# Batching the modulation rows of a two-layer diffusion block, four weight tiles to one accumulator copy

## The reference, cut to what matters

```python
def adaln(cond, w_mod, b_mod):
    return jnp.split(jax.nn.silu(cond) @ w_mod + b_mod, 6, axis=-1)

for l in range(DEPTH):
    sh1, sc1, g1, sh2, sc2, g2 = [m[:, None, :] for m in adaln(c, w_mod[l], b_mod[l])]
    csh1, csc1, cg1, csh2, csc2, cg2 = adaln(c_ctx, w_mod[l], b_mod[l])
    a_lat = rmsnorm(h, norm1_g[l]) * (1.0 + sc1) + sh1
    ...                     # token mixer: Fourier branch and state-space branch, gates, w_out
    h = h + g1 * o_lat
    f_lat = rmsnorm(h, norm2_g[l]) * (1.0 + sc2) + sh2
    h = h + g2 * channel_mixer(l, f_lat, ...)   # layer 0: dense SwiGLU; layer 1: top 2 of 8 experts
    ...                     # layer 0: the same for the context z, with csh1 to cg2
return rmsnorm(h, final_g)
```

## Time and profile before

| what | value |
|---|---|
| median of 3 runs | 2270.03 us (2267.54 to 2272.53) |
| the profiled execution's own time | 2270.69 us |
| its span in the profile | 2268.9 us |
| TensorE busy (products) | 2145.1 us, 95% of the span |
| DVE busy | 1400.2 us, 62% |
| ACT busy | 932.0 us, 41% |

### The profile page before, as it was taken

The page is one execution under the profiler, slowest core; times in us unless marked ns, Lnnn a source line. Parts: engine busy times, 40 slices in busy tenths (PEclk is TensorE's granted clock), DMA queues, the critical chain, the costliest instruction groups (busy, mean ns, idle before and its releaser), DMA issues.

```text
span 2268.9 us, 26156 instructions
## 1 busy us (share of the span) xinstructions
PE 2145.1 (95%) x10092; PEld 1618.4 (71%) x10092; DVE 1400.2 (62%) x1857; ACT 932.0 (41%) x839; POOL 0.2 (0%) x4
## 2 busy tenths in 40 slices
PE   4999989898999999899997999999999999999995
PEld 1455475345777777668986888888888888888884
DVE  5566516744222323418036889888888888888885
ACT  1212102111221222111004776767676766767673
POOL 0000000000000000000000000000000000000000
PEclk9999968998999999999697999999999999999997
DMA  8413574521435441357325999999898999999893
GB/s 355 112 75 149 172 171 179 183 74 37 182 143 194 164 194 48 133 159 176 97 108 215 359 348 355 353 335 377 330 374 325 369 341 360 350 338 378 325 374 150
DMA packets 84588, 536.49 MB, mean 236 GB/s; under 512 B 23040, under 2 KB 50304, under 8 KB 52992
## 3 DMA queue, kind: packets, MB, share of 16 engines
q1 hardware_dynamic: 62688, 513.89, 61.9%
q10 hardware_dynamic: 21792, 21.01, 2.8%
HBM read 516.59 MB, written 18.28 MB: 236 GB/s over the span
## 4 chain that ended last, share of the span: by engine, by line
PE 91%; DMA 4%; DVE 3%; issue 1%; ACT 1%; SPq 0%; DVEq 0%; ACTq 0%
PE ps L1486 20%; PE ps L1799 14%; PE ps L1800 14%; PE ps L1809 13%; PE ps L1495 6%; PE ps L1499 6%; PE ps L1502 5%; PE ps L1633 2%; PE ps L1422 2%; DMA bps<-BWs 2%; PE ps L1731 2%; PE ps L1753 1%; PE ps L1618 1%; DMA brt<-in_brt 1%; PE ps L1745 1%
## 5 line engine op out<-in xcount | busy, mean ns | idle before, releaser
L1326 DVE TENSOR_TENSOR WL<-mring,WH 128x2048 fp32r<-128x2048 f32 x340 | 763.6, 2288 | 111.9 <-ACT WH L826 111.4
L826 ACT ACTIVATE WH<-mring 128x2048 fp32r<-128x2048 f32 x340 | 632.6, 1913 | 142.2 <-PE ps L1809 130.2
L1799 PE MATMUL ps<-WH,XGh 128*128 128x512 f32 x896 | 358.2, 400 | 6.4 <-issue 3.9
L1800 PE MATMUL ps<-WH,XGl 128*128 128x512 f32 x896 | 349.9, 391 | 0.0
L1486 PE MATMUL ps<-aT,ring 128*128 128x512 f32 (+1 forms) x768 | 274.5, 518 | 12.4 <-ACT aT L707 12.4
L1486 PEld LDWEIGHTS ps<-aT,ring 128*128 128x128 f32 x768 | 147.8, 194 | 133.4 <-issue 122.0
L1809 PE MATMUL ps<-WL,XGh 128*128 128x512 f32 x896 | 221.5, 389 | 0.0
L1799 PEld LDWEIGHTS ps<-WH,XGh 128*128 128x128 f32 x896 | 168.9, 188 | 42.0 <-issue 5.1
L1809 PEld LDWEIGHTS ps<-WL,XGh 128*128 128x128 f32 x896 | 168.2, 188 | 34.9
L1800 PEld LDWEIGHTS ps<-WH,XGl 128*128 128x128 f32 x896 | 169.0, 189 | 33.6
L1151 DVE TENSOR_TENSOR ringl<-ring,FWH 128x4096 fp32r<-128x4096 f32 (+2 forms) x19 | 73.4, 3863 | 185.4 <-ACT FWH L693 185.4
(11 more groups left out here) (241 smaller groups left out, 2252.3 us busy)
## 6 DMA issues: line engine op xcount, KB each, us to landing
mring<-in_moe_gate SPq DMA_DIRECT2D x58, 2048.0 KB, 9.5
mring<-in_moe_up SPq DMA_DIRECT2D x57, 2048.0 KB, 9.7
mring<-in_moe_down SPq DMA_DIRECT2D x56, 2048.0 KB, 9.5
ring<-in_w_mod SPq DMA_DIRECT2D x24, 2048.0 KB, 8.3
ring<-in_w_in SPq DMA_DIRECT2D x12, 2048.0 KB, 11.8
ring<-in_ffn_gu SPq DMA_DIRECT2D x11, 2048.0 KB, 10.2
cks<-CW ACTq DMA_DIRECT2D x16, 512.0 KB, 3.3
ring<-cks SPq DMA_DIRECT2D x4, 2048.0 KB, 14.6
```

The lines of the kernel that those rows point to most:

```text
L826: nc.scalar.activation(WH[buf][:, o], mring[t % MRING][:, o], ACT.Copy).then_inc(high_done, 1)
L1326: V.tensor_tensor(WL[buf][:, o], mring[t % MRING][:, o], WH[buf][:, o].bitcast(F32), ALU.subtract).then_inc(low_done, 1)
L1799: mm(out_, ah, WH[buf][:, o:o + 512], start=(first and q == 0), stop=False)
L1800: mm(out_, al, WH[buf][:, o:o + 512], start=False, stop=False)
```

## The change

The selector and the sums are widened from two rows to eight. `silu4` holds four copies of the two condition columns, the i-th at columns 2i and 2i + 1 of an otherwise zero block of eight. Tile t uses block t mod 4 as stationary operand (128 x 8), so its two result rows land in rows 2(t mod 4) and 2(t mod 4) + 1 of each column group, and it adds zero to the others. The first tile of four starts the accumulation and the fourth ends it. ACT copies bank 2 once for four tiles, and one set of four turn products with a 128 x 8 selector makes the 32 columns. `mrow` has one buffer where it had two. DVE clears `silu4` at the start, and ACT applies `silu` four times, once into each block. The waits are counted in fours.

```diff
@@ constants @@
-        c[:, C_SEL + j] = p % 32 == j
+    c[:, C_SEL:C_SEL + 8] = (p[:, None] % 32) == np.arange(8)[None, :]
@@ tiles @@
-        mrow = sb(top, "mrow", [P, 2, 512])
+        mrow = sb(top, "mrow", [P, 512])
+        silu4 = sb(early, "silu4", [P, KD, 4, 8])
@@ ACT @@
-            nc.scalar.activation(silu_c[:], silu_c[:], ACT.Silu).then_inc(silu_c_ready, 1)
+            act.wait_ge(mod_bank_zero, 1)
+            for i in range(4):
+                last = nc.scalar.activation(silu4[:, :, i, 2 * i:2 * i + 2], silu_c[:], ACT.Silu)
+            last.then_inc(silu_c_ready, 1)
             def mod_rows(t):
+                if t % 4 < 3:
+                    return
                 act.wait_ge(mod_rows_done, t + 1)
-                if t >= 2:
-                    act.wait_ge(mod_cols_done, t - 1)
-                nc.scalar.activation(mrow[:, t % 2, :], ps[:, 2, :], ACT.Copy).then_inc(mod_rows_taken, 1)
+                if t >= 4:
+                    act.wait_ge(mod_cols_done, t // 4)
+                nc.scalar.activation(mrow[:], ps[:, 2, :], ACT.Copy).then_inc(mod_rows_taken, 1)
@@ DVE @@
+            link(V.memset(silu4[:], 0.0))
             link(V.memset(ps[:, 2, :], 0.0))
...
-                dve.wait_ge(mod_cols_done, hi)
+                dve.wait_ge(mod_cols_done, hi // 4)
@@ TensorE, mod_sums @@
-                if t:
-                    pe.wait_ge(mod_rows_taken, t)
+                if t and t % 4 == 0:
+                    pe.wait_ge(mod_rows_taken, t // 4)
...
-                    last = mm(ps[g:g + 2, 2, :], silu_c[:, k, :], wv[:, k, :],
-                              start=(k < 4), stop=(k >= 4), skip_group_check=True)
+                    last = mm(ps[g:g + 8, 2, :], silu4[:, k, t % 4, :], wv[:, k, :],
+                              start=(t % 4 == 0 and k < 4), stop=(t % 4 == 3 and k >= 4), skip_group_check=True)
@@ TensorE, mod_turn @@
-                pe.wait_ge(mod_rows_taken, t + 1)
-                if t in MOD_BATCH:
-                    pe.wait_ge(mod_cols_taken, MOD_BATCH.index(t) + 1)
+                if t % 4 < 3:
+                    return
+                pe.wait_ge(mod_rows_taken, t // 4 + 1)
+                if t - 3 in MOD_BATCH:
+                    pe.wait_ge(mod_cols_taken, MOD_BATCH.index(t - 3) + 1)
+                cols = ps[:, 3, 8 * t - 24:8 * t + 8].rearrange("p (t q c) -> p q t c", t=4, q=4)
                 for q in range(4):
-                    last = mm(ps[:, 3, 8 * t + 2 * q:8 * t + 2 * q + 2], mrow[:, t % 2, P * q:P * q + P],
-                              con[:, C_SEL:C_SEL + 2], start=True, stop=True)
+                    last = mm(cols[:, q], mrow[:, P * q:P * q + P],
+                              con[:, C_SEL:C_SEL + 8].rearrange("p (t c) -> p t c", c=2), start=True, stop=True)
                 last.then_inc(mod_cols_done, 1)
```

More of the change, by code:

```diff
@@ L64 @@
 C_CS, C_CN, C_SN, C_E16, C_MC, C_SEL = 640, 896, 1408, 1920, 1936, 1938
-C_N = 1940
+C_N = 1946
 def constants():
```

## The result

| | before | after |
|---|---|---|
| median (6 runs each, side by side) | 2268.49 us (2266.41 to 2272.53) | 2250.57 us (2248.65 to 2256.67) |
| ratio | | 0.9923, 95% interval 0.9908 to 0.9937 |
| profiled execution's own time | 2270.69 us | 2256.67 us |
| its span | 2268.9 us | 2254.9 us |

The change makes the kernel faster by 17.9 us. I had forecast 11.4 us, with 2254.0 us as the low end of the range: the sign was right and the size was not. Two later measurements of the same kernel gave 0.9913 and 0.9926.

What follows compares the result with a forecast made beforehand. TensorE was taken to bound the kernel wherever it has no idle time. SwiGLU 7.1, mixer 2.4 and start 1.9 us sum to 11.4 us, for a median of 2258.6 us, range 2254.0 to 2266.0 (8 in 10).

Steps and rivals of the forecast that it cites:

- What bounds the kernel: Whole kernel: TensorE, busy 95% of the span, bounds it wherever it has no idle time.
- the dense SwiGLU: Turns 12 to 23, no idle time on TensorE: nine removed turns at 0.79 us each give 7.1 us.
- The mixer: Layer 0's mixer: turns 4, 5 and 6 give 2.4 us; turns 8, 9 and 10, near waits, give 0.
- The first rival: Mixer wait at 242, 305 or 406 us hangs on an unmoved DMA, only the SwiGLU pays: 2262.9 us, 15%.
- The start: Tiles 0 to 3, clock rising at about 38.1 us: gain 1.9 us, between 0.8 and 2.6.
- the upper end: Start: clock rises early in sums 2, tile 3's landing at 36.8 us holds sums 3 back; gain 2.6 us.
- The four mode switches: Start: four changes of the array's tiling go with the turns, some 0.4 us more than counted.
- What is added: Wider loads (5 ns each, at most 1.9 us), wider turns, four silu operations, clearing and changed waits: taken as 0.
- The sum: Whole kernel: 7.1 + 2.4 + 1.9 = 11.4 us gained, median 2258.6 us.
- only to ask about the clock: Narrow products from 128.39 us, with waits between, might fall to the low clock: +8 us, 2266.6 us, 10%.
- the unknown costs of the edit: Whole kernel: bounds on uncertain terms put the gain between 5.8 and 14.8 us, 2264.2 to 2255.2 us.

Runs made afterwards that it cites:

- g1: Kernel before plus 48 dummy passes of tile 1 ahead of sums 1 to warm the clock and 40 tiny products after the sum of squares: 2268.34 us, ratio 0.9999.
- f2: Kernel before with the change's setup and all sums 8 columns wide, every copy and turn kept: 2265.29 us, ratio 0.9980.
- f1: Kernel before with the change's setup alone (`silu4` and wide selector), no tile batched: 2266.40 us, ratio 0.9988.
- h1: Changed kernel plus 20 tiny products (40 passes) after the first sum of squares, giving the E products their old code place: 2256.62 us, ratio 0.9950.
- the first set: The changed kernel again, and e1, e2 and e3, each with one part of the change; the parts gained 12.6, 6.2 and 10.4 us, the whole 20.2.
- e2: Kernel before with only tiles 0 to 3 batched (turns 0, 1 and 2 removed, the start): 2262.83 us, ratio 0.9966.
- e3: Kernel before with only tiles 4 to 11 batched (turns 4, 5, 6, 8, 9, 10 removed, the mixer): 2258.56 us, ratio 0.9954.
- e1: Kernel before with only tiles 12 to 23 batched (nine turns removed, all in the dense SwiGLU): 2256.40 us, ratio 0.9944.
- h4: Changed kernel plus 43 tiny products (86 passes) after the first sum of squares: 2251.45 us, ratio 0.9920.
- f3: Changed kernel with four dummy products at each of the 18 removed turns, ACT's copies still removed: 2282.81 us, ratio 1.0048 to the kernel before.
- g4: f3 plus 43 tiny products (86 passes) after the first sum of squares: 2261.73 us, ratio 0.9971 to the kernel before.
- g3: Kernel before plus only 43 tiny products (86 passes) after the first sum of squares: 2261.98 us, ratio 0.9981.
- h2: Kernel before plus 64 tiny products (128 passes, a whole code block) after the first sum of squares: 2269.77 us, ratio 1.0010.
- g2: Changed kernel plus dummy sums of tile 1 ahead of sums 1 and 40 tiny products after the sum of squares: 2252.52 us, ratio 0.9931.

## Why the prediction was too small

**What bounds the kernel, and the dense SwiGLU: right.** Nine turns at 0.79 us gave 7.1 us in every profile that had them removed, with no idle time and sums still 1.84 us.

**The mixer: right.** Turns 4 and 5 gave 53.5 - 51.6 = 1.9 us, turn 6 gave 0.9, together 2.8 where I had 2.4. Turns 8 and 9 were lost as forecast, in waits that grew from 2.20 to 2.83 and from 9.24 to 10.51 us; turn 10's came in with a wait of 6.79 us instead of 7.25, too small a thing to say more about. The first rival, a wait that hangs on a DMA that doesn't move, didn't come about.

**The start: mis-sized.** 1.9 us forecast, 3.0 in the profiled execution (and so the first E product 128.39 - 122.59 = 5.8 us earlier and not 3.5, another 0.8 of it from the low-clock stretch before 75 us). I had put the rise of the clock at the same moment as before, 38.1 us. In all seven profiles without turns it came before 35: sums 1 and 2 took 4.9 to 6.4 us together where I had 7.0, and then tile 3's landing was the bound. I had this case as the upper end (2.6 us). In the median it weighs little, though: with the turns in, the rise is early in half of the profiles, and g1, which has it early, showed no gain.

The page that I cited on this point says that the clock's points of judgement run freely (the Trainium skill, TensorE: Matmul & The Clock Gate, What's actually happening). The two kinds of start in kernels with the same start fit that. The four mode switches that I weighed there, 0.4 us, can't be told from the clock's part.

**What is added: right.** 5 ns more for each load, as estimated from the earlier trace rows, and none of it in the time (f2 against f1).

**The sum: right for what it counts.** 11.4 us forecast, 10.0 and 12.0 measured at equal place, and h1, which has the change with the place taken out, reads 2256.6 where I had said 2258.6.

**The step that failed is one that isn't in the sum.** I took it that removing instructions moves nothing but time, and so put the place of the code at nothing, without a reason. I read the wait of 2.22 us "issue" between 64-column products in the earlier trace rows and used it only to ask about the clock. I didn't ask what it was waiting for, nor look at the row behind it. Both waits go with the fetch of code, and 40 passes fewer ahead of them merge two into one. What the runs showed in place of nothing is 4 to 6 us: 1.4 to 2.5 us in the E stage, and most of the rest in layer 1's low-clock stages. My range covered the unknown costs of the edit, and this was a cost of something that the edit merely shifts; the median of 2250.57 us lies 3.4 us below its low end.

**What stays open.** What sets the form of layer 1's stages (above), and the parts' surplus in the first set. e2 (by work and place 1.9 to 3.5 plus 4 to 6, measured 4.1 to 11.3) and e3 (2.8 plus up to 6, measured 6.8 to 14.1) fit within their intervals; e1, whose E products are cut at 117 and which removes 7.1 us, gained 12.6 (8.6 to 16.8), so 1.5 us at least beyond it. It also moves 72 passes ahead of everything behind the SwiGLU, but h4 moved that too, by 86, and showed nothing.

## What to carry to other kernels

A small product between products of a TensorE that never idles is worth its start-to-start time (nine turns: 7.1 us forecast and measured), and that can be read off before anything is built; next to a wait for another engine or a transfer it is worth nothing. But when a profile shows waits with no releaser between short products, or just behind a loop's edge, count the passes between them: if they are 128, the place of the code is part of the time, and any edit ahead of them, even one that adds idle products, can gain or lose a few us (here an estimated 4 to 6 of 2268, and 21 between f3 and g4). Before crediting an edit with its whole gain, run it once more with the removed instructions replaced by idle ones in a place that hides them.

## What the hardware showed that I hadn't expected

- TensorE's code arrives in transfers of 16384 bytes, 128 passes of load and product. 64-column products use one up in 3.95 us and then, at most cuts, wait 0.9 to 3.3 us; the 278 us of 512-column products in the SwiGLU show no such wait.
- Adding 86 passes of idle work made the kernel 0.19% faster (g3) and f3 0.9% faster (g4); adding 128 made no difference (h2).
- A loop's edge cost 0.5 to 2.1 us on TensorE in all kernels that I looked at there, and in one place of the code (f3) 3.7 to 4.2 us more, each with 6.8 us at half clock: 19 us over three edges.
- Two stages of layer 1, in which TensorE does the same products in every kernel here, took 184.1 to 184.3 us in six profiles and 185.4 to 187.9 in the other thirteen. In before and g3 the difference goes with a granted clock two hundredths lower in both stages.
- Warming TensorE's clock ahead of a stage can cost more than it brings when the stage then ends in a wait: the sum of squares took 10.11 us instead of 7.11 (g2).
